# Gate and value products of a feed-forward stage: a 512-column product with the high weight part, its halves of a bank added afterwards

## The reference, cut to what matters

```
def conv_ffn(x, w_gate, w_val, conv_w, conv_b, w_down):
    h = causal_dwconv(x @ w_gate, conv_w) + conv_b      # 3 taps along the positions
    return (jax.nn.silu(h) * (x @ w_val)) @ w_down
...
x = layer_norm(ALPHA * x + conv_ffn(x, *ffns[layer]), *ln2[layer])
```

## Time and profile before

| | us |
|---|---|
| median of 3 runs | 3455.18 (3450.88 to 3457.72) |
| profiled execution: span, the only time the page gives for it | 3452.7 |
| TensorE busy, products | 3364.0 (97%) |
| TensorE busy, weight loads | 3308.8 (96%) |
| VectorE / ScalarE busy | 2253.6 (65%) / 1615.7 (47%) |

### The profile page before, as it was taken

The page is one execution under the profiler, slowest core; times in us unless marked ns, Lnnn a source line. Parts: engine busy times, 40 slices in busy tenths (PEclk is TensorE's granted clock), DMA queues, the critical chain, the costliest instruction groups (busy, mean ns, idle before and its releaser), DMA issues.

```text
span 3452.7 us, 68659 instructions
## 1 busy us (share of the span) xinstructions
PE 3364.0 (97%) x30038; PEld 3308.8 (96%) x30038; DVE 2253.6 (65%) x3653; ACT 1615.7 (47%) x2337; POOL 58.8 (2%) x78
## 2 busy tenths in 40 slices
PE   8999999999999899999999999999999999999997
PEld 8999999999998888999999999998999999999997
DVE  6666555557677787796666655687656966666455
ACT  5444444444455534364444444564443644444443
POOL 1000000000000000000000000001000000000000
PEclk9999999999999999999999999999999999999998
DMA  6555555555564322356555566543444565555663
GB/s 238 174 175 176 184 177 173 182 176 178 175 198 147 98 87 93 105 180 195 192 195 193 191 193 190 188 154 108 153 135 135 169 201 193 194 195 190 188 202 125
DMA packets 162492, 586.36 MB, mean 170 GB/s; under 512 B 18128, under 2 KB 18128, under 8 KB 161936
## 3 DMA queue, kind: packets, MB, share of 16 engines
q1 hardware_dynamic: 160560, 574.01, 50.9%
q0 software_dynamic: 1632, 7.96, 0.7%
HBM read 579.80 MB, written 2.10 MB: 169 GB/s over the span
## 4 chain that ended last, share of the span: by engine, by line
PE 57%; DVE 6%; ACT 1%; issue 1%; POOL 0%; ACTq 0%; DVEq 0%; POOLq 0%
PE bank L2142 17%; PE bank L2144 17%; PE bank L2143 17%; DVE pairs L2935 1%; PE bank L2346 1%; PE bank L2359 1%; DVE xs L3051 1%; DVE xs L3049 1%; PE bank L2157 0%; PE bank L2158 0%; PE bank L2159 0%; DVE xr L2939 0%; DVE right L3399 0%; ACT pairs L2612 0%; ACT xs L2663 0%
## 5 line engine op out<-in xcount | busy, mean ns | idle before, releaser
L2142 PE MATMUL bank<-xr,pairs 128*128 128x256 f32 (+1 forms) x5888 | 1661.4, 282 | 33.2 <-DVE pairs L2935 27.6
L2144 PE MATMUL bank<-xr,pairs 128*128 128x256 f32 (+1 forms) x5888 | 1638.6, 278 | 0.0
L2143 PE MATMUL bank<-xr,pairs 128*128 128x256 f32 (+1 forms) x5888 | 1638.5, 278 | 0.0
L2612 ACT ACTIVATE pairs<-raw 128x1024 fp32r<-128x1024 f32 x1106 | 1142.8, 1042 | 950.5 <-PE bank L2144 750.6
L2935 DVE TENSOR_TENSOR pairs<-raw,pairs 128x1024 fp32r<-128x1024 f32 x1106 | 1308.9, 1202 | 348.2 <-ACT pairs L2612 342.1
L2142 PEld LDWEIGHTS bank<-xr,pairs 128*128 128x128 f32 x5888 | 1114.0, 189 | 45.8 <-DVE pairs L2935 30.6
L2143 PEld LDWEIGHTS bank<-xr,pairs 128*128 128x128 f32 x5888 | 1112.7, 189 | 1.4
L2144 PEld LDWEIGHTS bank<-xr,pairs 128*128 128x128 f32 x5888 | 1112.3, 189 | 0.0
L2142 PE MATMUL bank<-parts,pairs 128*128 128x256 f32 x1792 | 496.5, 277 | 0.4 <-DVE parts L2939 0.4
L2143 PE MATMUL bank<-parts,pairs 128*128 128x256 f32 x1792 | 495.0, 276 | 0.0
L2144 PE MATMUL bank<-parts,pairs 128*128 128x256 f32 x1792 | 495.0, 276 | 0.0
(11 more groups left out here) (602 smaller groups left out, 3047.2 us busy)
## 6 DMA issues: line engine op xcount, KB each, us to landing
raw<-in_w_in SPq DMA_DIRECT2D x176, 512.0 KB, 4.8
raw<-in_gate SPq DMA_DIRECT2D x176, 512.0 KB, 5.6
raw<-in_val SPq DMA_DIRECT2D x176, 512.0 KB, 4.2
raw<-in_down SPq DMA_DIRECT2D x160, 512.0 KB, 4.4
raw<-in_l_w_in SPq DMA_DIRECT2D x144, 512.0 KB, 3.9
raw<-in_w_out SPq DMA_DIRECT2D x64, 512.0 KB, 4.7
raw<-in_l_w_out SPq DMA_DIRECT2D x64, 512.0 KB, 3.9
raw<-in_v_in SPq DMA_DIRECT2D x48, 512.0 KB, 4.7
```

The source lines that it names most:

```text
L2142: mm(o, wh[:, q, :], rh[:, k, :], start=begin and q == 0, stop=False)
L2143: mm(o, wh[:, q, :], rl[:, k, :], start=False, stop=False)
L2144: last = mm(o, wl[:, q, :], rh[:, k, :], start=False, stop=end and q == c - 1)
L2612: e.activation(pair_of(n)[0], v3(raw_of(n), widths[n] // slices[n]), ACT.Copy).then_inc(*hi_made(n))
```

## The change

Tiles t = 6 to 43 of both feed-forward stages are computed by `col_parted`. For each block there are two products instead of three: wh by (xh, xl) side by side, 512 columns, into both halves of a bank (`joined` is the access pattern that puts xl behind xh); then wl by xh, 256 columns, added into the second half. A tile's sum is the first half plus the second half. The gate tile and the value tile get a bank each.

Behind the products, `parted_tile` takes the place of `act_tile`. ScalarE copies the first half of the gate bank to SBUF (`gate_high`), VectorE adds the second half (`gate_sum`), and the three instructions of the convolution then read SBUF. After the activation VectorE multiplies it with the first half and with the second half of the value bank and adds the two (`val_gate`). `gate_high` is issued one piece into the value tile. `col_settled` and `settle` are gone, and the scratch area of the stage has 6 instead of 5 times 256 columns, for the two buffers of the gate sums.

```
+        def col_parted(n, bk, rhs, k0, begin, end, ready):
+            (wh, wl), (rh, rl), c, o2 = pair_of(n), rhs, widths[n] // 128, v3(bk.view, 2)
+            w.wait_ge(*lo_made[n])
+            if begin:
+                w.on(bk.after)
+            for q in range(c):
+                k = k0 + q
+                w.on(ready[q])
+                mm(o2, wh[:, q, :], joined(rh[:, k, :], rl[:, k, :]), start=begin and q == 0, stop=False)
+                last = mm(o2[:, 1, :], wl[:, q, :], rh[:, k, :], start=False, stop=end and q == c - 1)
+            last.then_inc(*used(n))
...
+        def parted_tile(j):
+            j.s = yield from buf(gb)
+            do("gate_high", j)
+            yield
+            j.b = yield from buf(hb)
+            do("gate_conv", j)
+            banks.put(j.bg, (vec, "gate_sum", j.id))
+            gb.put(j.s, (vec, "ffn_conv", j.id))
+            yield
+            j.g = yield from buf(tb)
+            do("ffn_silu", j)
+            while j.mv is None:
+                yield
+            yield
+            do("val_gate", j)
+            banks.put(j.bv, (vec, "val_low", j.id))
+            hb.put(j.b, (vec, "ffn_u", j.id))
...
         for t in range(FF):
...
-            else:
-                while len(banks.free) < 2:
-                    pump()
-                bk = banks.get()
-                p2 = v3(bk.view, 2)
-                if t == 9:
-                    spare = banks.get()
-                    n = load(f"gate{l}", t, 0)
-                    do("col_settled", n, p2[:, 0, :], X2, [last.at(q) for q in range(8)], bk.after, spare)
...
-                    col_tile(p2[:, 0, :], both(f"gate{l}", t), X2, last.at, bk)
-                m = col_tile(p2[:, 1, :], both(f"val{l}", t), X2, last.at, bk)
-            side.append(act_tile(t, bk, m))
+            j = Job()
+            j.id, j.l, j.t, j.mv = next(ids), l, t, None
+            j.bg = mbank()
+            j.mg = col_tile_parted(both(f"gate{l}", t), X2, last.at, j.bg)
+            side.append(parted_tile(j))
+            j.bv = mbank()
+            j.mv = col_tile_parted(both(f"val{l}", t), X2, last.at, j.bv)
...
+        def gate_high(j):
+            w.on([j.mg])
+            w.on(j.s.after)
+            e.activation(j.s.view, j.bg.view[:, 0:T], ACT.Copy).then_inc(*act("gate_high", j.id))
...
+        def gate_conv(j):
+            s, b, l, t = j.s.view, j.b.view, j.l, j.t
+            w.wait_ge(*act["gate_high", j.id])
+            e.tensor_tensor(s, s, j.bg.view[:, T:2 * T], ADD).then_inc(*vec("gate_sum", j.id))
+            w.on(j.b.after)
+            w.wait_ge(*vec["gate_sum", j.id])
+            e.tensor_scalar(b, s, VC(f"cw2_{l}", t), VC(f"cb_{l}", t), MUL, ADD).then_inc(*vec("conv2", j.id))
...
+        def val_gate(j):
+            g, b = j.g.view, j.b.view
+            w.on([j.mv])
+            w.wait_ge(*act["silu", j.id])
+            e.tensor_tensor(b, g, j.bv.view[:, 0:T], MUL).then_inc(*vec("val_high", j.id))
+            e.tensor_tensor(g, g, j.bv.view[:, T:2 * T], MUL).then_inc(*vec("val_low", j.id))
+            w.wait_ge(*vec["val_low", j.id])
+            e.tensor_tensor(g, g, b, ADD).then_inc(*vec("ffn_u", j.id))
```

More of the change, by code:

```diff
@@ L384, in two, with joined @@
         return ap.unsqueeze(1).broadcast_to([128, 2, T])
+    def joined(high, low):
+        return bass.AP(high.tensor, high.offset, [high.ap[0], (low.offset - high.offset, 2), high.ap[-1]])
     def g4(ap):
@@ L576, in col_tile, with col_tile_parted @@
                 pump()
+            k += c
+        return (used, n)
+    def col_tile_parted(keys, rhs, ready, bk):
+        k = 0
+        for key in keys:
+            n = load(*key)
+            c = widths[n] // 128
+            do("col_parted", n, bk, rhs, k, key is keys[0], key is keys[-1], [ready_at(ready, k + q) for q in range(c)])
+            pump()
             k += c
@@ L1684, in ffn @@
         ut = [None] * FF
-        buf5 = v3(take(5 * T), 5)
-        hb = Slots([Buf(buf5[:, i, :]) for i in range(2)])
-        tb = Slots([Buf(buf5[:, i, :]) for i in range(2, 4)])
+        buf6 = v3(take(6 * T), 6)
+        hb = Slots([Buf(buf6[:, i, :]) for i in range(2)])
+        tb = Slots([Buf(buf6[:, i, :]) for i in range(2, 4)])
+        gb = Slots([Buf(buf6[:, i, :]) for i in range(4, 6)])
         tiles_ = [(w + str(l), t) for t in range(6) for w in ("gate", "val")]
@@ L1711, in act_tile @@
             tb.put(j.g, *ut[t])
+        def parted_tile(j):
[15 more added lines that the diff above has]
+            hb.put(j.b, (vec, "ffn_u", j.id))
+            yield
+            s = split_job(u[0][:, j.t, :], u[1][:, j.t, :], j.g.view, (vec, "ffn_u", j.id))
+            do("part_hi", s)
+            yield
+            do("part_lo", s)
+            ut[j.t] = s.there
+            tb.put(j.g, *ut[j.t])
         for t in range(FF):
@@ L2122, in _build @@
         elif st != "norm":
-            upart = phase(5 * T, 2 * FF * T)
+            upart = phase(6 * T, 2 * FF * T)
             norm = ffn(int(st[3]), norm)
@@ L2159, in row @@
                     last = mm(o, lh[:, k, ms], wl[:, q, :], start=False, stop=k == KT - 1)
[L2160 to L2181, removed]
             last.then_inc(*used(n))
@@ L2581, in ret_pv @@
             mm(ps[:, 128:T], s["v"][:, 1, hh, :], s["A"][:, T:T + 128], start=False, stop=True).then_inc(*pe("ret_pv", j.pr, hh))
-        steps = dict(col_settled=col_settled, norm_cols=norm_cols, col=col, row=row, rms_sq=rms_sq, ln_first=ln_first, norm_sums=norm_sums, scores=scores,
+        steps = dict(norm_cols=norm_cols, col=col, col_parted=col_parted, row=row, rms_sq=rms_sq, ln_first=ln_first, norm_sums=norm_sums, scores=scores,
                      p_turn=p_turn, pv=pv, rope_mm=rope_mm, kpe_turn=kpe_turn, ukv_k=ukv_k, ukv_v=ukv_v, uq=uq, head_sum=head_sum,
@@ L2916, in scalar_program @@
                      gd_v1=gd_v1, gd_out=gd_out, silu_tanh=silu_tanh, o_sq=o_sq, ret_qk=ret_qk, ret_v=ret_v,
-                     ret_out=ret_out, ffn_silu=ffn_silu)
+                     ret_out=ret_out, gate_high=gate_high, ffn_silu=ffn_silu)
         for name, args in plan:
@@ L3379, in ffn_conv @@
                                    op1=ADD).then_inc(*vec("ffn_conv", j.id))
+        def gate_conv(j):
[5 more added lines that the diff above has]
+            e.tensor_scalar(b, s, VC(f"cw2_{l}", t), VC(f"cb_{l}", t), MUL, ADD).then_inc(*vec("conv2", j.id))
+            w.wait_ge(*vec.now())
+            e.scalar_tensor_tensor(out=b[:, 1:T], in0=s[:, 0:T - 1], scalar=VC(f"cw1_{l}", t), in1=b[:, 1:T], op0=MUL,
+                                   op1=ADD).then_inc(*vec("conv1", j.id))
+            w.wait_ge(*vec.now())
+            e.scalar_tensor_tensor(out=b[:, 2:T], in0=s[:, 0:T - 2], scalar=VC(f"cw0_{l}", t), in1=b[:, 2:T], op0=MUL,
+                                   op1=ADD).then_inc(*vec("ffn_conv", j.id))
+        def val_gate(j):
[6 more added lines that the diff above has]
+            e.tensor_tensor(g, g, b, ADD).then_inc(*vec("ffn_u", j.id))
         def ffn_gate(j):
@@ L3571, in vector_program @@
                      rk_state=rk_state, rk_out=rk_out, center=center, rk_norm=rk_norm, ffn_conv=ffn_conv,
-                     ffn_gate=ffn_gate, mix1_zero=mix1_zero, conv_taps=conv_taps, conv_out=conv_out, row_beta=row_beta,
+                     ffn_gate=ffn_gate, gate_conv=gate_conv, val_gate=val_gate, mix1_zero=mix1_zero, conv_taps=conv_taps, conv_out=conv_out, row_beta=row_beta,
                      row_gate=row_gate, row_sums=row_sums, row_turn=row_turn, row_factors=row_factors, kq_norm=kq_norm,
```

## The result

The changed kernel takes 3485.05 us (3482.07 to 3488.96, 4 runs) against 3454.97 us: 0.9% slower, ratio 1.0087 with a 95% interval of 1.0075 to 1.01. Forecast were 3434 us and a range of 3414 to 3453.

What follows compares the result with a forecast made beforehand. TensorE's instruction count and spacing were taken to bound the kernel. Blocks of 333.5 ns instead of 340.0 save 10.7 us a stage: 3452.7 - 2 x 10.7 = 3431.3, plus 2.5 to the median, 3434 us; range 3414 to 3453.

Steps and rivals of the forecast that it cites:

- What bounds the kernel: Whole kernel: count and spacing of TensorE's instructions set the time; TensorE busy 97% in products, other engines run with slack.
- The two spacings: Stretch from tile 6 to the down projection: 256-column products start 0.1133 us apart when fast, 0.1178 us when slow.
- the check of the sum: Old stretch: 306 slow products, 3342 fast ones and 1.35 us for small products make 416.1 us against 416.2 measured.
- The long product: 512-column fp32r product in each block of tiles 6 to 43: taken at 215.5 ns, hiding the next load wholly.
- The short product: 256-column product behind each 512-column one: expected at the slow value each time, 118 ns.
- The upper bound: Changed stretch: all columns at the slow cost, 3 x 117.8 = 353.3 ns a block, 429.6 us.
- the row of 0.215: Earlier trace at 883.22 to 883.65: plain fp32 products of 256 columns, 0.215 us apart, 2.2 ns above 213.3.
- The small products ... need no term of their own: Removed small products (1.35 us) and the slow start counted as inside the stretch's 416.2 us, with no separate term.
- Rival 4: Slow pattern stays: 342.3 ns a block in the stretch, down projection +9.5 us a stage, 3474 us; chance 0.08.
- Rivals 1 to 3: Stretch blocks of 328.8, 324.5 and 340.0 ns, for 3422, 3412 and 3450 us; chances 0.22, 0.08 and 0.14.
- rival 3: Stretch: gap belongs to columns, 512-column product behaves as two of 113.3 ns; block stays 340.0 ns, 3450 us; chance 0.14.
- The work behind the products: VectorE's added 1.25 us a tile and ScalarE's copy in the stretch hide beside TensorE; counted at nothing.

Runs made afterwards that it cites:

- experiment 1: Kernel before the change with the three small products of tile 9 removed: 3486.24 us, ratio 1.0094, runs from 3474.93 to 3499.16.
- experiment 9: Changed kernel with one product a block, bfloat16 or fp32r, 512 or 256 columns by tile: 216 ns against 234 ns at 512 columns.
- experiment 5: Kernel before's three products a block and small products up to tile 9, changed kernel's two products from tile 10: 3489.02 us, ratio 1.01.
- experiment 2: Changed kernel with the three small products put back in the gate tile of t = 9: 3490.54 us, ratio 1.0103.
- experiment 3: Changed kernel with its 512-column product cut into two of 256, without small products: 3492.67 us, runs from 3465.53 to 3504.81.
- experiment 4: Changed kernel with its 512-column product cut into two of 256 and the three small products put back: 3455.11 us, ratio 1.0002.
- experiment 11: Kernel before the change with the three small products in tile 6 instead of tile 9: 3450.71 us, ratio 0.9987.

## Why the prediction was wrong, step by step

**What bounds the kernel** held: TensorE's spacing, no wait for another engine. **The two spacings** held, and so did the check of the sum: all fast is 413.44, all slow 429.65, measured in single stages of experiment 1.

**The long product is the step that failed.** "I take 215.5 ns for the long product", from the plain fp32 products of the earlier trace rows. It measured 235.0 beside a short one and 233.4 alone. The row was of another kind of product, plain fp32, which takes half as many columns in that time. "No row shows an fp32r product of 512 columns" holds for the rows written down, but the trace of the kernel before has twelve such products. In the attention stage, at L2281 to L2283, they follow each other at clock 1.00:

```profile
1078.31 0.39 PE L2281 MATMUL bank<-pairs,parts 128*128 128x512 f32 x1
1078.54 0.39 PE L2282 MATMUL bank<-pairs,parts 128*128 128x512 f32 x1
1078.76 0.39 PE L2283 MATMUL bank<-pairs,parts 128*128 128x512 f32 x1
1078.99 0.39 PE L2281 MATMUL bank<-pairs,parts 128*128 128x512 f32 x1
```

From the first to the last of the twelve they are 229 ns apart in the mean. In the prediction's own sum, 229 + 118 = 347 ns a block make 422 us a stretch, 5.8 more than before instead of 10.7 less: about 3470 with the slow start of the down projection. That is still 15 us short of the measured time, but slower, as it came. The rule weighed there (the Trainium skill, "TensorE: Matmul & The Clock Gate", section "Back-to-back issue gap", N / 2.4 + 2.5) gives 215.8 and 109.2; bfloat16 in experiment 9 stands at 216 and 109, in agreement. For fp32r from 320 columns on the traces lie 7 to 9% above it, and the traces decide. Neither of the two sources that agreed in the prediction was a measurement of fp32r products.

**The short product** was right at 118 (118.3), and so was its reason, the slow value behind a long product (118 behind the first long one of experiment 5, from a fast start). **The upper bound** of the text, 3 x 117.8 = 353.3 ns and 429.6 us, is what came, to 0.1 us. I had left it out of the range, since "this needs the long product to behave as two with nothing gained, which the row of 0.215 speaks against". One row of another kind of product was let stand against a bound; at that bound the sum is 3455.2 + 2 x 13.4 + 2 x 1.4 = 3485, the measured time.

**"The small products ... need no term of their own"** was wrong as well. Experiment 1 prices their removal at up to 429.65 - 416.2 = 13.4 us a stretch, with up to 1.4 and 8.0 more in the down projection before and behind the sums. In the changed kernel itself it costs nothing on top, since the long products are slow with or without them (experiments 2 and 5): the missing term was a real risk of the edit, but not what made the forecast wrong. The two causes don't add: the long product always leaves the stretch at 353.3 ns a block, the missing small ones do in the stages that are entered slow, and mending one alone (experiments 2 and 3) gives nothing reliable back. Only both together do (experiment 4).

**The rivals.** Rival 4 had the right sign and half of the mechanism, the latch; its price (342.3) took the row of 0.215 as its base and was short by 11 ns. Its down projection that stays slow, 9.5 us a stage, did not come in the changed kernel, where only the 1.4 us up to the sums did; in one stage of experiment 1 it came. Rivals 1 to 3 all rested on a long product that is fast or can be; rival 3 was right that the cost goes by columns, and took the fast value for it.

**The work behind the products** at nothing: right (experiment 4). VectorE rose by 49 us in the stretch, 1.3 a tile, as costed.

## What to carry to other kernels

Fewer instructions and weight loads gained nothing on TensorE here, where the stream of columns is what binds. Before a product is made wider, take the rate from a product of the same operand type: one of another type with the same clock count was 9% off here, while twelve of the right type stood in the trace of the kernel before, in another stage. When an edit removes an instruction whose result nobody uses, run the kernel without that instruction first; here that alone costs the whole difference on the median. Where runs of one kernel spread by 24 us or more, as in experiments 1 and 3, one profiled run is one draw. And where a bound from the rows is ruled out by a single row, leave it in the range.

## What the runs showed of the hardware that was not expected

- An fp32r stream of 320 to 512 columns takes 0.45 to 0.46 ns a column at the full granted clock (229 to 237 ns for 512 columns, by place and neighbours), a bfloat16 one 216 ns for 512 columns. At the granted clock of 0.50 the fp32r streams of 384 and 448 columns take just their clock count, 320 and 373 ns. Why is open.
- Products of 256 fp32r columns, back to back, keep one of two spacings, 113.3 or 117.8 ns, for thousands of products: 3648 in one stage of experiment 1 at the one, 3648 in the other at the other. Which it is changed from stage to stage of the same kernel. Behind the last of the three small products the products of 256 columns were fast in all eight stages profiled with them (the kernel before, experiments 4, 5 and 11). Why they do, what decides the pattern without them, and why 256 columns can be fast when the rate above would give 117, is open.
- Moving the start of the 512 columns changes a block by up to 4.4 ns of 353.3, and starts 256 bytes apart give the same. Whether another place of the weights would do more wasn't tried.
